# A two-layer decoder trunk on one core: expert rows are added to the output in HBM by indirect DMA instead of being scattered by TensorE

## What is computed

```python
def swiglu(h, w_gate, w_up, w_down):
    return (jax.nn.silu(h @ w_gate) * (h @ w_up)) @ w_down

def moe_ffn(h, w_router, w_e_gate, w_e_up, w_e_down):
    logits = jnp.einsum('bsd,de->bse', h, w_router, preferred_element_type=jnp.float32)
    top_vals, top_idx = lax.top_k(logits, TOP_K)
    top_w = jax.nn.softmax(top_vals, axis=-1)
    combine = jnp.sum(jax.nn.one_hot(top_idx, N_EXPERTS, dtype=jnp.float32) * top_w[..., None], axis=-2)
    combine = combine.astype(h.dtype)
    y = jnp.zeros_like(h)
    for e in range(N_EXPERTS):
        y = y + combine[..., e:e + 1] * swiglu(h, w_e_gate[e], w_e_up[e], w_e_down[e])
    return y
...
            x = x + moe_ffn(h, w_router[i], w_exp_gate[i], w_exp_up[i], w_exp_down[i])
```

## Time and profile before

| what | value |
|---|---|
| median of the runs | 1085.41 us (1085.15 to 1085.47, 3 runs) |
| span of the profiled execution, first to last instruction | 1083.6 us |
| TensorE busy (matmuls) | 1071.3 us, 99% |
| VectorE busy | 833.5 us, 77% |
| ScalarE busy | 675.9 us, 62% |
| GpSimd busy | 73.4 us, 7% |
| moved by DMA | 250.19 MB |
| expert stage | from about 670 us to the end |

### The profile page before, as it was taken

How to read it: one execution, slowest core, us unless ns; L and a number is a source line. 1 busy time by engine, 2 the same in 40 slices (tenths; PEclk the granted TensorE clock), 3 DMA queues, 4 the chain that set the end, 5 groups by cost and what they waited for, 6 DMA issues and landing times.

```text
span 1083.6 us, 16940 instructions
## 1 busy us (share of the span) xinstructions
PE 1071.3 (99%) x6443; PEld 918.3 (85%) x6443; DVE 833.5 (77%) x1166; ACT 675.9 (62%) x959; POOL 73.4 (7%) x119
## 2 busy tenths in 40 slices
PE   8999999999999999999999999999999999999997
PEld 6978788889999998979888878888888888888885
DVE  5679776986554646567956888899889898989896
ACT  5676746555344434756755547886767677777764
POOL 5003330000000000000622000000000000000000
PEclk9999999999999999999999999999999999999999
DMA  9553544567456445355254547899999899999992
GB/s 281 170 192 92 173 138 155 171 237 267 147 175 228 156 165 173 108 178 172 89 193 132 179 157 243 298 353 320 344 321 380 297 357 321 382 329 362 345 349 106
DMA packets 146933, 250.19 MB, mean 231 GB/s; under 512 B 6478, under 2 KB 105892, under 8 KB 146852
## 3 DMA queue, kind: packets, MB, share of 16 engines
q1 hardware_dynamic: 144784, 246.37, 66.7%
q10 hardware_dynamic: 2068, 2.72, 0.7%
HBM read 248.02 MB, written 1.05 MB: 230 GB/s over the span
## 4 chain that ended last, share of the span: by engine, by line
PE 93%; DVE 4%; ACT 1%; issue 1%; DMA 1%; DVEq 0%; ACTq 0%
PE PS L720 27%; PE PS L1268 11%; PE PS L1269 11%; PE PS L1270 11%; PE PS L1066 6%; PE PS L1065 6%; PE PS L1067 6%; PE PS L825 2%; PE PS L744 2%; PE PS L926 1%; DVE m_lo L2023 1%; PE PS L1217 1%; PE PS L1205 1%; DVE scr L2308 1%; DVE big L2300 1%
## 5 line engine op out<-in xcount | busy, mean ns | idle before, releaser
L457 DVE TENSOR_TENSOR w_lo<-ring,w_hi 128x1536 fp32r<-128x1536 f32 (+1 forms) x191 | 309.2, 1632 | 96.2 <-ACT w_hi L448 95.8
L448 ACT ACTIVATE w_hi<-ring 128x1536 fp32r<-128x1536 f32 (+1 forms) x192 | 264.5, 1387 | 121.2 <-PE PS L1067 71.8
L1495 ACT ACTIVATE m_hi<-ring 128x512 fp32r<-128x512 f32 (+2 forms) x256 | 157.7, 631 | 126.2 <-PE PS L720 122.1
L2023 DVE TENSOR_TENSOR m_lo<-ring,m_hi 128x512 fp32r<-128x512 f32 (+2 forms) x256 | 182.6, 743 | 57.1 <-ACT m_hi L1495 55.1
L1268 PE MATMUL PS<-w_hi,hTe 128*96 128x384 f32 (+1 forms) x384 | 125.1, 326 | 0.0
L1269 PE MATMUL PS<-w_hi,hTe 128*96 128x384 f32 (+1 forms) x384 | 123.9, 323 | 0.0
L1270 PE MATMUL PS<-w_lo,hTe 128*96 128x384 f32 (+1 forms) x384 | 123.8, 322 | 0.0
L720 PE MATMUL PS<-m_hi,h_hi 128*128 128x512 f32 (+3 forms) x320 | 119.4, 373 | 1.4 <-DVE m_lo L2023 1.4
L720 PE MATMUL PS<-m_hi,h_lo 128*128 128x512 f32 (+3 forms) x320 | 115.1, 360 | 0.0
L720 PE MATMUL PS<-m_lo,h_hi 128*128 128x512 f32 (+3 forms) x320 | 115.0, 359 | 0.0
L1065 PE MATMUL PS<-h_hi,w_hi 128*128 128x256 f32 x352 | 99.9, 284 | 0.0
(11 more groups left out here) (356 smaller groups left out, 2188.7 us busy)
## 6 DMA issues: line engine op xcount, KB each, us to landing
ring<-in_w_in_dram SPq DMA_DIRECT2D x39, 1024.0 KB, 5.1
ring<-in_w_exp_gate_dram SPq DMA_DIRECT2D x48, 768.0 KB, 6.3
ring<-in_w_exp_up_dram SPq DMA_DIRECT2D x48, 768.0 KB, 7.8
ring<-in_w_exp_down_dram SPq DMA_DIRECT2D x24, 1536.0 KB, 8.4
ring<-in_w_branch_dram SPq DMA_DIRECT2D x12, 1024.0 KB, 5.1
ring<-in_w_ffn_gate_dram SPq DMA_DIRECT2D x12, 768.0 KB, 5.6
ring<-in_w_ffn_up_dram SPq DMA_DIRECT2D x12, 768.0 KB, 6.2
ring<-in_w_ffn_down_dram SPq DMA_DIRECT2D x6, 1536.0 KB, 6.9
```

Source lines behind the costliest of these rows:

```text
L448: act.activation(split_parts(u, j)[0], ring[:, i % NSLOT, w0:w0 + words], ACT.Copy)\
L457: dve.tensor_tensor(lo, ring[:, (j // 2) % NSLOT, w0:w0 + words], hi.bitcast(F32), SUB).then_inc(sem(f"lo_ready{b}"), 1)
L1495: act.activation(hi, raw, ACT.Copy).then_inc(sem("m_hi_ready"), 1)
L2023: dve.tensor_tensor(lo, raw, hi.bitcast(F32), SUB).then_inc(sem("m_lo_ready"), 1)
```

## The change

The output is no longer collected in `x_tok`. Once the last mixer has finished, GpSimd stores the residual (2 x 512 KB) straight to the output in HBM. Each expert then makes its 96 rows ready in SBUF, already multiplied by the router's weight, and GpSimd adds them to the output with one indirect DMA that adds in HBM (`compute_op=ADD`): row s of `ye` goes to token `row_of[s, e]`. The DMA of an expert waits for the one before it. Expert 7 goes in two DMAs, one per 512 columns.

Every slot must name a token of its own, also an unused one. So `pall` gives each slot of each expert one token (the tokens that the expert doesn't have fill the slots left over, with weight 0), and 16 small matmuls (`row_info`, behind half 15 of expert 0) carry weight (two parts) and token number to the slots. The matmuls of `prepare`, `scatter` and `last_scatter`, the additions to `x_tok`, `identr`, `selT`, `ye_hi`, `ye_lo` and the four stores at the end are gone.

```diff
-EXPERT_AFTER = {3: [("gu", 0), ("scatter", 0)], 4: [("scatter", 1)], 6: [("tr", 0)], 7: [("gu", 1)], 11: [("tr", 1)], 13: [("gu", 2)],
+EXPERT_AFTER = {3: [("gu", 0)], 6: [("tr", 0)], 7: [("gu", 1)], 11: [("tr", 1)], 13: [("gu", 2)],
                 17: [("tr", 2)], 19: [("gu", 3)], 20: [("tr", 3)]}
+INFO_AFTER = 15
...
# TensorE
-            def scatter(r, e, n, part):
...
+            def row_info(r):
+
+                b, uses = aux_use(r, "info", 0)
+                pe.wait_ge(sem("pall_ready"), 2 * r + 2)
+                pe.wait_ge(sem("wsel_ready"), 1)
+                wait_aux_free(pe, b, uses)
+                for e in range(NE):
+                    for a in range(TT):
+                        mm = pe.matmul(PS[0:CAP, 4 + b, RW * e:RW * (e + 1)], pall[:, a, e, :], wsel[:, a, e, :],
+                                       start=(e == 0 and a == 0), stop=(a == TT - 1), skip_group_check=True)
+                mm.then_inc(sem(f"aux_full{b}"), 1)
...
# GpSimd, behind its last work of the mixer
+            for a in range(TT):
+                for c in range(2):
+                    _, _, free, n = use(DEPTH - 1, f"w{c}{a}")
+                    pool.wait_ge(free, n + 1)
+                pool.dma_start(y[:, a, :], x_tok[:, a, :]).then_inc(sem("residual_out"), 16)
+            pool.wait_ge(sem("residual_out"), 16 * TT)
+
+            def rows_added(r):
+
+                pool.wait_ge(sem("rows_known"), r + 1)
+                for e in range(NE):
+                    n = r * NE + e
+                    pool.wait_ge(sem("first_ready"), n + 1)
+                    if e < NE - 1:
+                        pool.wait_ge(sem("second_ready"), n + 1)
+                    if r or e:
+                        pool.wait_ge(sem("rows_added"), 16 * (ROWS_DONE * r + e))
+                    if e < NE - 1:
+                        pool.indirect_dma_start(out.rearrange("b t d -> (b t) d"), bass.IndirectOffsetOnAxis(row_of[0:CAP, e:e + 1], 0),
+                                                ye[0:CAP, e % 2, :], None, compute_op=ADD).then_inc(sem("rows_added"), 16)
+                        continue
+                    for c in range(2):
+                        if c:
+                            pool.wait_ge(sem("second_ready"), n + 1)
+                        pool.indirect_dma_start(out.rearrange("b t (c d) -> (b t c) d", c=2), bass.IndirectOffsetOnAxis(half_row[0:CAP, c:c + 1], 0),
+                                                ye[0:CAP, e % 2, c * 512:(c + 1) * 512], None, compute_op=ADD)\
+                            .then_inc(sem("rows_added"), 16)
+                pool.wait_ge(sem("rows_added"), 16 * ROWS_DONE * (r + 1))
+
+            rows_added(0)
+            pool.wait_ge(sem("passes_known"), 1)
+            npass = pool.value_load(npi[0:1, 0:1], min_val=1, max_val=PASSES)
...
# ScalarE: the first columns
+            def rows_out(r, e, n):
...
+                if e > 1:
+                    act.wait_ge(sem("rows_added"), 16 * (ROWS_DONE * r + e - 1))
...
+                act.activation(ye[0:CAP, e % 2, 0:512], PS[0:CAP, 6, :], ACT.Copy, scale=rw[0:CAP, e:e + 1]).then_inc(sem("first_ready"), 1)
...
# VectorE: the other columns, and what the slots hold
+            def rows_out(r, e, n):
...
+                wait_used(dve, expert_unit(n), HALVES - 1)
+                dve.tensor_scalar(ye[0:CAP, e % 2, 512:1024], PS[0:CAP, 7, :], rw[0:CAP, e:e + 1], None, MUL)\
+                   .then_inc(sem("second_ready"), 1)
+
+            def row_info(r):
...
+                info = PS[0:CAP, 4 + b, 0:RW * NE].rearrange("p (e s) -> p e s", s=RW)
+                dve.tensor_reduce(rw[0:CAP, :], info[:, :, 0:2], AX.X, ADD)
+                dve.tensor_copy(row_of[0:CAP, :], info[:, :, 2])
+                for c in range(2):
+                    dve.tensor_scalar(half_row[0:CAP, c:c + 1], info[:, NE - 1, 2:3], 2.0, float(c), MUL, ADD)\
+                       .then_inc(sem(f"aux_free{b}") if c else sem("rows_known"), 1)
```

More of the change, by code:

```diff
@@ L64 @@
 DB = 4
-COLUMN_ORDER = (0, 2, 1, 3)
+ROWS_DONE = NE + 1
 def expert_after(e, j):
     what = list(EXPERT_AFTER.get(j, ()))
+    if e == 0 and j == INFO_AFTER:
+        what.append(("info", 0))
     if e in BATCH_IN and j in BATCH_AFTER:
@@ L101, in place_aux @@
             for what, x in expert_after(e, j):
-                if what == "scatter":
-                    for c in (2 * x, 2 * x + 1):
-                        take(("scatter", e, c), c % 2)
+                if what == "info":
+                    take(("info", 0), 0)
                 elif what == "tr":
@@ L1243, in row_scales @@
                     mm.then_inc(sem("totals_full"), 1)
[L1245 to L1263, removed]
             def expert(r, e, n):
@@ L1338, in expert @@
                             turn(r, e, n, x)
[L1339 to L1342, removed]
+                        elif what == "info":
+                            row_info(r)
                         elif what == "gather":
@@ L1453, in _ @@
                                channel_multiplier=-1).then_inc(sem("tri_ready"), 1)
+            y = out.rearrange("b (a p) d -> p (b a) d", p=P)
+            for a in range(TT):
[27 more added lines that the diff above has]
+            npass = pool.value_load(npi[0:1, 0:1], min_val=1, max_val=PASSES)
+            for r in range(1, PASSES):
+                with pool.If(npass > r):
+                    rows_added(r)
         @block.scalar
@@ L1847, in expert @@
                             tokens(r, BATCH_IN[e], g)
-                        elif what == "scatter" and e == 0:
-                            for c in (2 * g, 2 * g + 1):
-                                b, uses = aux_use(r, "scatter", 0, c)
-                                wait_aux_full(act, b, uses)
-                                act.activation(selT[0:CAP, 2 * c:2 * c + 2, :], two(PS[0:CAP, 4 + b, :]), ACT.Copy)\
-                                   .then_inc(sem(f"aux_free{b}"), 1)
                     if j < HALVES and not (j < EARLY and isinstance(n, int) and n == 0):
@@ L2506, in expert @@
                                               hdT_hi[:, g0:g0 + gn, :].bitcast(F32), SUB).then_inc(sem(f"aux_free{b}"), 1)
-                        elif what == "scatter" and e > 0:
-                            added(r, e, g)
+                        elif what == "info":
+                            row_info(r)
                         elif what == "gather":
@@ L2552, in one_pass @@
                 e0, ne = BATCHES[0]
-                if not isinstance(r, int):
-                    dve.wait_ge(sem("stored"), 64)
                 if not isinstance(r, int):
```

167 lines of the change are left out of this document (76 added, 91 removed).

## The result

The changed kernel takes 1075.88 us (median of 4 runs, 1075.25 to 1076.71) against 1085.44 us (1085.15 to 1085.52). The ratio is 0.9914, 95% interval 0.99 to 0.9928. The forecast was 1075.7 us. That near a hit is in part luck: three terms of the sum were off, a fourth loss was not in it, and the errors nearly cancel.

What follows compares the result with a forecast made beforehand. TensorE, busy 99% of the span, was taken as the bound, with VectorE and DMA close to their limits. Terms -15.5 - 0.1 + 2.3 + 3.6 + 0 + 0 = -9.7 us took 1085.4 to 1075.7 us, range 1068 to 1083.

Steps and rivals of the forecast that it cites:

- The scatter leaves TensorE: Expert stage: seven experts each lose 2.22 us of scatter matmuls on TensorE, all on the path, -15.5 us.
- Prepare out, `row_info` in: Expert 0, TensorE: two parts of prepare (1.4 us) go, 16 small matmuls (1.31 us) come, net -0.1 us.
- VectorE's eight steps: Expert 0 before half 14: 3.1 us of new VectorE steps, 0.8 covered, stall TensorE at `hdT_lo`, +2.3 us.
- The loads have to keep up: Experts 2, 4, 5, 6: loads plus row additions need 48.1 us against TensorE's 47.2, giving back +3.6 us.
- The residual's store: GpSimd's 1 MB store at about 658 to 668 us delays loads first used over 15 us later: 0 (to +1).
- the new waits: Copies for expert e wait until the addition of expert e-2 has landed, with 47 us for it: worth nothing.
- Landings of over 10 us: Listed sign that the forecast is wrong: additions taking over 10 us to land.
- The end: From last columns to end of span, 8.7 us before: 5.0 to 11.9 us now, middle taken as 0.
- lowest case: Sum of all the low bounds: 1085.4 - 15.5 - 0.6 - 3.7 = 1065.6 us.
- TensorE stays the only bound: Rival: additions too small to be felt, VectorE's steps overlap, all but the tail gained, 1069.8 us; chance 0.2.
- The loads have nothing left to give: Rival: experts without a gather stay at 49.4 us, only experts 1, 3, 7 gain, 1081.0 us; chance 0.17.
- Each adding row holds its DMA engine: Rival: adding rows block their DMA engines in sequence, a loss from 3.7 us an addition, 1096 us; chance 0.12.

Runs made afterwards that it cites:

- first experiment: Changed kernel with slot places and the two pall comparisons moved to halves 18 to 20 of expert 0, row_info behind half 20: 1073.08 us.
- all three repairs: Changed kernel with places and comparisons later in expert 0, token numbers made late, and number of passes read before the additions: 1070.28 us.
- three additions: Changed kernel with the rows of experts 0 to 6 each added three times, GpSimd waiting for each addition: 1091.15 us.
- kernel that adds twice: Changed kernel with the rows of each expert but the last added twice, GpSimd waiting for the first addition: 1084.04 us.
- sixteen rows: Changed kernel with the additions of experts 0 to 6 moving only 16 of their 96 rows: 1076.97 us.
- number of passes read first: Changed kernel with GpSimd reading the number of passes ahead of its additions instead of behind its last wait: 1074.33 us.
- token numbers late: Changed kernel with GpSimd's iota moved ahead of `tri` and VectorE's three token-number operations moved behind `most_rows`: 1074.16 us.
- last expert in whole rows: Changed kernel with the last expert's rows added as whole rows in one DMA behind both halves of `ye`: 1076.77 us.

## Why the prediction came out

- **The scatter leaves TensorE, -15.5:** right. Experts 1 to 7 give 15.6 us, and leaving the scatter out alone gives 15.6 us.
- **Prepare out, `row_info` in, -0.1:** the new block takes 1.30 us (712.71 to 714.01), as the 1.31 us of its nearest row. But part of what `prepare` leaves is not gained. TensorE now comes to a half of `exp_down` 1.4 us earlier (counted from the first matmul of expert 0), ahead of VectorE, and waits 0.53 us for `hdT_lo` at 691.79 (0.70 us from start to start). The kernel before has no such wait. The eight steps aren't its cause: they come later, and the wait is there, 0.53 us at the same half, also where they were moved (first experiment, and all three repairs). That the missing `prepare` is the cause wasn't tested by itself.
- **VectorE's eight steps, +2.3 (bounds 0 and 3.1):** the mechanism was right, the place and the size of the wait too (2.10 us). The term was mis-sized: 1.5 us more come from the granted clock behind the stall. The upper bound held no cost of a stall beyond its length. With the second wait above this is 4.5 of the 4.6 us that expert 0 lost (2.25 and 0.70 us from start to start, 1.5 for the clock).
- **The loads have to keep up, +3.6 (bounds 0 and 6):** wrong; it measured 0. The step that failed is "49.4 x 1.00 / 1.06 = 46.6 us at the least". It takes 49.4 us of busy time as an amount of work that stays. By queue, the loads of an expert show 2.83 us for a MB in the kernel before and 2.74 us with three additions, where the queues are full. With these rows 17.3 MB need an estimated 17.3 x 2.74 / 1.06 = 44.7 us, and an addition 1.98 / 1.06 = 1.9 us. That gives 46.6 us with one addition, under TensorE's 47.1, then 48.5 with two and 50.3 with three; experts 5 and 6 took 48.5 and 48.7 us with two, 50.8 and 51.1 with three. So the price of an addition, 1.5 us, was too low, and the loads' own need was set nearly 2 us too high. Why the same bytes show less busy time in fuller queues stays open.
- **The residual's store, 0, and the new waits, 0:** right. Additions land 12.5 us behind the start of their issue, far under an expert's 47 us. Landings of over 10 us were listed as a sign that the forecast is wrong; they are not one, since 5.54 us of it is GpSimd's issue and nobody waits for the rest.
- **The end, 0 (bounds -3.7 and +3.2):** +0.6, in the middle as taken. Of the parts, the issue measured 1.42 us, not 0.7, and stands there twice in a row. The 3 us of the upper bound for the register load and two branches are shown by no run; reading the number of passes first saved about 0.5 us.
- **The stages ahead of the experts** were not in the sum at all, +1.7. Four tiny operations at 16 and 57 us were passed over because TensorE wasn't near them.

The errors: 3.6 too much for the loads against 2.4 (expert 0), 1.7 (early) and 0.6 (end) too little. That they nearly cancel is luck. (The sum of the lowest case takes off 0.6 us where the term's own bound is 0.5, which moves nothing.) The rival "TensorE stays the only bound" had the mechanism of experts 1 to 7 right, and its 1069.8 us is what the kernel reaches once the three side costs are mended (1070.28). "The loads have nothing left to give" falls with the windows of 47.10 us. The Trainium skill (DMA: Bandwidth & Descriptors, Specifications) gives a core about 358 GB/s from HBM, by which no such expert could load its 17.3 MB in under 48.3 us. This case's trace doesn't agree: 17.3 MB in 47.10 us are 367 GB/s. The same page of the Trainium skill (Bandwidth) says that this figure is what each of two cores of a pair gets when both stream, and here one core runs, so it was no bound for this kernel. "Each adding row holds its DMA engine" falls too: it needed 3.7 us an addition to turn the change to a loss, and an addition costs an estimated 1.9 us of full queues, 2.2 to 2.4 us from two to three.

## What to carry to other kernels

Price a stall of the bounding engine at more than its length, and look at windows of a few microseconds behind it, because slices of the page hide a short fall of the clock. Before adding work to a resource whose share is near its highest value, measure its room by adding the same work once more: here the first addition was free and the second cost 8.2 us. A busy share alone doesn't give that room: read it by queue, and beside the bytes. Tiny operations in an early stage are part of a change too; here 0.2 us of shift cost nearly 2 us where two engines work side by side, and with the operations moved behind that stretch the experts began as early as before (670.35 us, 670.55 before).

## What was not expected of the hardware

- **GpSimd's issue of an indirect DMA takes 1.42 to 5.54 us, and it seems to go by what VectorE does.** It isn't set by the rows (5.41 us with 16) nor by their length (1.42 us for 4 KB). The kernel that adds twice has both values within 13 us. VectorE's and GpSimd's timelines there:

```profile
779.90 1.74 DVE L466 TENSOR_TENSOR w_lo_last<-ring,w_hi_last 128x1536 fp32r<-128x1536 f32 x1
781.56 5.16 DVE L466 TENSOR_TENSOR w_lo<-ring,w_hi 128x1536 fp32r<-128x1536 f32 x3
...
792.92 0.45 DVE L2520 TENSOR_TENSOR hdT_lo<-PS,hdT_hi 128x288 fp32r<-128x288 f32 x1
793.83 1.76 DVE L466 TENSOR_TENSOR w_lo<-ring,w_hi 128x1536 fp32r<-128x1536 f32 x1 [0.46 <-ACT w_hi L457]
```

```profile
780.75 5.53 POOL L1448 DMA_INDIRECT out_dram<-ye,row_of  x1 [37.18 <-DVE ye L2486]
793.59 1.42 POOL L1451 DMA_INDIRECT out_dram<-ye,row_of  x1 [7.31 <-DMA out_dram<-ye,row_of]
```

  The short one begins in a gap of VectorE (793.37 to 793.83), the long one in an unbroken run of splits. Its end less 1.42 us is 784.86, when the third split of the run had to wait for ScalarE (whose `w_hi` ended at 784.93). That GpSimd gets in only when VectorE's splits pause fits these rows; it was not tested by itself. Values in between occur where the splits end sooner: 2.52 us at 1036.60 in the same trace ends, less 1.42 us, at 1037.70, and VectorE goes from a split to `hdT_lo` at 1037.74, without a pause. The long issue costs nothing here, because the landing isn't waited for.
- **Behind the same stall of 2.1 us the clock falls in some executions and not in others.** It was 0.50 for 3.4 us in the traces of the changed kernel, of sixteen rows and of the number of passes read first (seen also with the token numbers late). It stayed at 1.00 behind that stall in the traces of the last expert in whole rows and of the kernel that adds twice. And it can fall without a stall, at 662.0 us in one trace. The runs spread over 1.46 us with the stall (changed kernel), 0.67 us with it moved (first experiment) and 0.14 us with all three repairs.
- **An adding DMA of 393 KB** lands 12.5 us behind the start of its issue beside the loads, and one of 196 KB 4.8 us at the idle end.
